# Last down projection of a two-block transformer: 16 of its 44 weight chunks as seven block products

## The reference

```python
        f = rms_norm_2(h, ffn_norm_g[i])
        h = h + (jax.nn.silu(f @ ffn_w1[i]) * (f @ ffn_w3[i])) @ ffn_w2[i]
        h = h + (p[i] @ pl_w_up[i]) * jax.nn.sigmoid(h @ pl_w_gate[i])
    return rms_norm_2(h, final_norm_g)
```

## Time and profile before

| what | value |
|---|---|
| median of 3 runs | 2418.42 us (2418.24 to 2418.65) |
| span of the profiled execution, first to last instruction | 2417.2 us |
| PE busy | 2404.8 us, 99% |
| DVE busy | 1389.7 us, 57% |
| ACT busy | 1170.4 us, 48% |
| first matmul of `down2`, of `pg2` | 2081.40 us, 2320.76 us |

### The profile page before, as it was taken

One profiled execution on the slowest core, in us unless ns is written; L12 is line 12 of the kernel. 1 busy time (PEld: TensorE's weight loads), 2 busy tenths in 40 slices (PEclk: granted clock), 3 DMA queues, 4 the chain that ended last, 5 costly groups with the idle time before them and its releaser, 6 DMA issues.

```text
span 2417.2 us, 27743 instructions
## 1 busy us (share of the span) xinstructions
PE 2404.8 (99%) x10956; PEld 2000.9 (83%) x10956; DVE 1389.7 (57%) x1192; ACT 1170.4 (48%) x1110; POOL 127.4 (5%) x138
## 2 busy tenths in 40 slices
PE   9999999999999999999999999999999999999998
PEld 8888888888888888888888888888888888888886
DVE  6877645656666666544666474664545445444446
ACT  5554554656656556333455464454343433433335
POOL 5000000001111011000000000000010100100000
PEclk9999999999999999999999999999999999999999
DMA  7566556587777778755698855776766767666663
GB/s 257 187 205 204 167 179 199 179 301 237 234 243 252 235 235 253 276 205 193 202 299 279 254 174 175 231 245 211 230 211 214 221 208 226 231 225 213 213 229 123
DMA packets 276834, 535.16 MB, mean 221 GB/s; under 512 B 12634, under 2 KB 47376, under 8 KB 275856
## 3 DMA queue, kind: packets, MB, share of 16 engines
q1 hardware_dynamic: 276304, 533.21, 68.0%
q10 hardware_dynamic: 448, 0.79, 0.1%
HBM read 495.15 MB, written 39.59 MB: 221 GB/s over the span
## 4 chain that ended last, share of the span: by engine, by line
PE 99%; ACT 1%; DVE 0%; DMA 0%; issue 0%; DVEq 0%; SPq 0%; ACTq 0%
PE ps L1462 31%; PE ps L1464 31%; PE ps L1463 31%; PE ps L1455 2%; PE ps L1456 1%; PE ps L1700 1%; PE ps L1438 0%; PE ps L1715 0%; DMA h<-in_x_dram 0%; ACT w_hi L819 0%; PE ps L1840 0%; PE ps L1684 0%; PE ps L1721 0%; PE ps L1751 0%; DVE w_lo L1898 0%; ACT g_work L984 0%
## 5 line engine op out<-in xcount | busy, mean ns | idle before, releaser
L1898 DVE TENSOR_TENSOR w_lo<-raw,w_hi 128x2048 fp32r<-128x2048 f32 x424 | 980.5, 2312 | 986.4 <-ACT w_hi L819 986.1
L819 ACT ACTIVATE w_hi<-raw 128x2048 fp32r<-128x2048 f32 x424 | 812.8, 1917 | 1207.7 <-PE ps L1464 1168.5
L1462 PE MATMUL ps<-w_hi,xa 128*128 128x512 f32 x1856 | 723.6, 390 | 0.0
L1464 PE MATMUL ps<-w_hi,xa 128*128 128x512 f32 x1856 | 722.2, 389 | 0.0
L1463 PE MATMUL ps<-w_lo,xa 128*128 128x512 f32 x1856 | 722.1, 389 | 0.0
L1462 PE MATMUL ps<-w_hi,g 128*128 128x512 f32 x1408 | 549.2, 390 | 0.0
L1464 PE MATMUL ps<-w_hi,g 128*128 128x512 f32 x1408 | 547.9, 389 | 0.0
L1463 PE MATMUL ps<-w_lo,g 128*128 128x512 f32 x1408 | 547.8, 389 | 0.0
L1464 PEld LDWEIGHTS ps<-w_hi,xa 128*128 128x128 f32 x1856 | 348.4, 188 | 72.7
L1462 PEld LDWEIGHTS ps<-w_hi,xa 128*128 128x128 f32 x1856 | 348.4, 188 | 72.4 <-DVE w_lo L1905 0.2
L1463 PEld LDWEIGHTS ps<-w_lo,xa 128*128 128x128 f32 x1856 | 348.4, 188 | 71.8
(11 more groups left out here) (315 smaller groups left out, 997.6 us busy)
## 6 DMA issues: line engine op xcount, KB each, us to landing
raw<-in_ffn_w_dram SPq DMA_DIRECT2D x132, 1024.0 KB, 5.2
raw<-in_w_in_dram SPq DMA_DIRECT2D x94, 1024.0 KB, 5.2
raw<-in_w_up_dram SPq DMA_DIRECT2D x88, 1024.0 KB, 5.9
raw<-in_w_down_dram SPq DMA_DIRECT2D x44, 1024.0 KB, 5.4
raw<-in_w_out_dram SPq DMA_DIRECT2D x32, 1024.0 KB, 5.1
raw<-in_w_pg_dram SPq DMA_DIRECT2D x16, 1024.0 KB, 7.2
raw<-in_pl_w_gate_dram SPq DMA_DIRECT2D x16, 1024.0 KB, 6.0
up_turned_rows<-h SPq DMA_DIRECT2D x22, 512.0 KB, 3.0
```

Of the source, the lines that this page charges most:

```text
L819: A(w_hi[j % SPLIT][:, :], raw[s][:, :], ACT.Copy).then_inc(sem("w_hi_ready"), 1)
L1462: mm(o, high, hi, start=begin, stop=False)
L1464: return mm(o, low, hi, start=False, stop=end)
L1898: V.tensor_tensor(w_lo[j % SPLIT][:, :], raw[j % RAW][:, :], w_hi[j % SPLIT][:, :].bitcast(F32), ALU.subtract).then_inc(sem("w_lo_ready"), 1)
```

## The change

Of the 22 chunks of `down2` and of `down2b`, chunks 3, 5, 7, ... 17 (eight in each phase) are multiplied by Strassen's scheme. A chunk is now two k-tiles by 1024 columns in every chunk of these phases (before: four k-tiles by 512 columns), that is a 2x2 grid of 128x512 weight blocks, and the two k-tiles by two halves of tokens are a 2x2 grid of 128x128 activation blocks. In Winograd's form of the scheme the grid product takes seven block products in place of eight: 21 matmuls in place of 24. The first of these products is summed in bank 4, others in 5, 6 and 7, and those that belong to one output only go straight into banks 0 to 2.

The block sums that the scheme needs are made in three places:

- Weight sums, for each of the 16 chunks on DVE: `early_sums` (1024 wide), `late_sums` (two of 512; one overwrites a block of `raw` in place), then ACT rounds the three sums (`sums_high`, 1536 wide) and DVE makes their low part (`low_sums`, 1536 wide). The rounding of the chunk itself now waits for the first of the late sums.
- Activation sums ("forms"), once for each of eight k-tile pairs, in steps 1 to 8 of `glu`: four sums of 128x128 on POOL, rounded on ACT, low part on POOL, put in DRAM by SP. In `down2` and again in `down2b` SP loads 512 KB of them for each seven-product chunk; PE waits for them after its second product.
- Output sums, once a phase: a copy on ACT, eight additions of 128x512 on DVE at chunks 17 and 18.

Because both halves of the columns now grow together, both are finished only at the end of a phase: `add_pair` takes the place of `add_rows`, and PE starts the next phase when the halves are read. `turn_h` of quarters 0 and 1 moves into `down2b`, quarters 2 and 3 to its end, their takes into `pg2`; the 2 MB of `take_second` moves from `down2` to `pg2`. Some semaphores are merged under common names.

In the diff below, the first `paired`, the wait and transfer of the forms and the three tables of puts and takes are SP's; `seven` is in ACT's `high`; `seven_products` is PE's; the rest is DVE's.

```diff
+SEVEN = {"down2": (3, 5, 7, 9, 11, 13, 15, 17), "down2b": (3, 5, 7, 9, 11, 13, 15, 17)}
...
+            def paired(ph, w, c0, at):
+                for j in range(plan[ph]["body"]):
+                    if j in at:
+                        at[j]()
+                    load(ph, 0, j, weight(w, 2 * j, 2, c0, 1024))
+                    if j - 2 in SEVEN[ph]:
+                        take_forms(ph, j - 2)
...
+                sp.wait_ge(sem("chunks_multiplied"), chunk_no(ph, 0, c - 4) + 1 if n >= 2 else plan[ph]["chunk"])
+                sp.dma_start(form_factors[ph][n % 2].bitcast(F32), forms_dram[:, first:first + 1024]).then_inc(sem(f"forms_landed{n % 2}"), 16)
...
-            columns("down2", [(w, 0), (w, 512)], 1024, kts=FT,
-                    at={6: lambda i: put_blocks(plan["glu"]["iters"]), 7: lambda i: take_blocks(plan["glu"]["iters"]),
-                        8: take_second,
-                        16: lambda i: put_h_blocks("pg2", 0), 17: lambda i: take_h_blocks("pg2", 0)})
-            columns("down2b", [(w, 1024), (w, 1536)], 1024, kts=FT,
-                    at={5: lambda i: put_h_blocks("pg2", 1), 6: lambda i: take_h_blocks("pg2", 1),
-                        16: lambda i: put_h_blocks("pg2", 2), 17: lambda i: take_h_blocks("pg2", 2)})
+            paired("down2", w, 0,
+                   at={6: lambda: put_blocks(plan["glu"]["iters"]), 7: lambda: take_blocks(plan["glu"]["iters"])})
+            paired("down2b", w, 1024,
+                   at={8: lambda: put_h_blocks("pg2", 0), 9: lambda: take_h_blocks("pg2", 0),
+                       12: lambda: put_h_blocks("pg2", 1), 13: lambda: take_h_blocks("pg2", 1)})
             columns("pg2", [(t["pl_w_gate_2"][0], 0), (t["pl_w_gate_2"][0], 512)], 1024, peel=2,
-                    at={5: at_step(0, lambda: put_h_blocks("pg2", 3)),
-                        6: both(at_step(0, lambda: take_h_blocks("pg2", 3)), load_final_row)})
+                    at={0: at_step(1, lambda: take_h_blocks("pg2", 3)), 2: at_step(1, take_second),
+                        6: at_step(0, lambda: put_h_blocks("pg2", 2)),
+                        7: at_step(0, lambda: (take_h_blocks("pg2", 2), put_h_blocks("pg2", 3))), 5: at_step(1, lambda: load_final_row(0))})
...
+                seven = ph in SEVEN and i == 0 and j in SEVEN[ph]
+                if seven:
+                    act.wait_ge(sem("sums"), 3 * seven_no(ph, j) + 2)
                 A(w_hi[j % SPLIT][:, :], raw[s][:, :], ACT.Copy).then_inc(sem("w_hi_ready"), 1)
+                if seven:
+                    act.wait_ge(sem("sums"), 3 * seven_no(ph, j) + 3)
+                    A(sums_high[ph], sums[seven_no(ph, j) % 2], ACT.Copy).then_inc(sem("sums_high"), 1)
...
+            def seven_products(ph, j, hi, lo):
+                three(4, early[:, 0:P], early[:, S:S + P], block_(hi, 0), block_(lo, 0), begin, end)
+                three(0, late[:, 0:P], late[:, S:S + P], block_(hi, 2), block_(lo, 2), False, False)
+                pe.wait_ge(sem(f"forms_landed{n % 2}"), landed_forms(ph, n))
+                three(6, *form(1), block_(hi, 1), block_(lo, 1), begin, end)
+                three(2, *form(3), block_(hi, 3), block_(lo, 3), False, False)
+                pe.wait_ge(sem("sums_low"), no + 1)
+                hi, lo = sums_high[ph], sums_low[no % 2]
+                three(5, *form(0), block_(hi, 0), block_(lo, 0), begin, end)
+                three(7, *form(2), block_(hi, 1), block_(lo, 1), begin, end)
+                return three(1, late[:, P:S], late[:, S + P:2 * S], block_(hi, 2), block_(lo, 2), False, False)
...
+            def early_sums(ph, c):
+                dve.wait_ge(sem(f"raw_landed{c % RAW}"), landed_count(ph, c))
+                dve.wait_ge(sem("chunks_multiplied"), chunk_no(ph, 0, c - 4) + 1 if n >= 2 else plan[ph]["chunk"])
+                V.tensor_tensor(sums[no % 2][:, 0:1024].rearrange("p (k n) -> p k n", k=2), blocks[:, 1],
+                                raw[c % RAW][:, 0:1024].rearrange("p (k n) -> p k n", k=2), ALU.subtract).then_inc(sem("sums"), 1)
...
+            def paired(ph, n, at):
+                done_at = SEVEN[ph][-1]
+                for j in range(plan[ph]["body"]):
+                    if j == plan[ph]["body"] - 1:
+                        add_pair(ph, n)
+                    low(ph, 0, j + SPLIT)
+                    if j + SPLIT in SEVEN[ph]:
+                        low_sums(ph, j + SPLIT)
+                    if j == 0:
+                        early_sums(ph, 3)
+                    if j + 3 in SEVEN[ph]:
+                        late_sums(ph, j + 3)
+                    if j + 4 in SEVEN[ph] and j:
+                        early_sums(ph, j + 4)
+                    if j == done_at:
+                        merge_products(ph, n)
+                    if j == done_at + 1:
+                        add_products(ph, n)
+                    if j in at:
+                        at[j]()
+            paired("down2", 0, {})
+            paired("down2b", 2, {3: lambda: turn_h("pg2", 0), 6: lambda: staged_low("pg2", 0), 7: lambda: turn_h("pg2", 1),
+                                 10: lambda: staged_low("pg2", 1), 21: lambda: (turn_h("pg2", 2), turn_h("pg2", 3))})
```

More of the change, by code:

```diff
@@ L133, in two_blocks_program @@
         cols = sb("cols", [P, 434])
+        with nc.sbuf_tensor("forms_work", [P, 1024], F32) as forms_work:
+            pass
+        with nc.sbuf_tensor("forms", [P, 1024], F32R) as forms:
+            pass
         ident = sb("ident", [P, P])
@@ L140, in two_blocks_program @@
         with nc.sbuf_tensor("ff", [P, 16, S], F32) as ff:
+            pass
+        with nc.sbuf_tensor("ff_r", [P, 16 * S], F32R) as ff_r:
             pass
@@ L549, in h_block_dram @@
             def h_block_dram(ph, q):
-                return turned_dram if (ph, q) == ("pg1", 3) else up_turned_dram
+                return turned_dram if (ph, q) in (("pg1", 3), ("pg2", 3)) else up_turned_dram
             def put_h_blocks(ph, q):
@@ L1196, in earlier_glu, with form_high, glu_sixth @@
                     glu_high(i - 1)
+            def form_high(e):
+                act.wait_ge(sem("forms_summed"), e * 3)
+                A(forms[:, 0:512], forms_work[:, 512:1024], ACT.Copy).then_inc(sem("forms_high"), 1)
+            def glu_sixth(i):
+                if isinstance(i, int) and i == 0:
+                    silu_gate(0)
+                elif not isinstance(i, int) or i - 1 in FORM_TILES:
+                    form_high(i - 1)
             def earlier(f, n=1):
@@ L1389, in _ @@
                 0: steps({1: lambda: row_squares("out", 1)}),
+                1: steps({0: lambda: staged_high("pg2", 2)}),
                 3: steps({0: last_staged_high, 1: lambda: sigmoid("pg2", 2)}),
@@ new lines, in landed_forms, with paired @@
+            def landed_forms(ph, n):
+                before = len(range(n % 2, len(SEVEN["down2"]), 2)) if ph == "down2b" else 0
+                return 16 * (before + n // 2 + 1)
+            def paired(ph, name):
+                for j in range(plan[ph]["body"]):
+                    pe.wait_ge(sem(name), j // 2 + 1)
+                    pe.wait_ge(sem("w_lo_ready"), chunk_no(ph, 0, j) + 1)
+                    products = seven_products if j in SEVEN[ph] else eight_products
+                    products(ph, j, w_hi[j % SPLIT][:, :], w_lo[j % SPLIT][:, :]).then_inc(sem("chunks_multiplied"), 1)
```

255 lines of the change are left out of this document (185 added, 70 removed).

## The result

| kernel | median, us | runs | ratio to before, 95% |
|---|---|---|---|
| before | 2418.33 (2417.97 to 2418.65) | 4 | |
| after | 2439.79 (2438.46 to 2441.42) | 4 | 1.0089 [1.0074, 1.0103] |

Forecast: 2421.0 us, range 2410 to 2427. The changed kernel is 21.5 us slower than before, outside the range. The profiled execution took 2441.42 us, its span is 2439.7 us against 2417.2 us.

A forecast was written before the change was run, and what follows sets the result against it. PE, busy 99% of the span, was taken as the bound. The terms, -10.9 + 2.4 + 9.2 + 1.9 = +2.6 us, were added to 2418.4 us, giving 2421.0 us; range 2410 to 2427, likeliest case 2418.7 to 2424.3.

The forecast's parts named there:

- 16 chunks x 3 matmuls x 0.2267 us = 10.9 us: Seven-product chunks of `down2` and `down2b`: the removed matmuls on PE save 10.9 us.
- Rival D: PE doesn't get shorter because the new matmuls, through more banks, come slower than 0.2267 us: 2430 us, chance 0.03.
- The steady pairs: Pairs of chunks in the phases' steady part: PE takes 10.20 us, DVE's loop 9.92, so PE leads and nothing is lost.
- the 2.4 us of small stalls: DVE work at phase starts (0.26 us), phase ends (0.58) and transposes of quarters 0 and 1 (1.57) adds 2.4 us.
- rival C: DVE becomes the bound if each step has 0.1 us more, in steady pairs: about 2428 us, chance 0.07.
- Where SP is held up: `down2b`: puts waiting for transposes delay loads, so PE waits for forms at chunks 7 and 11, 4.6 us each, 9.2 us.
- Rival A: Transfers land in time and both forms stalls in `down2b` vanish: -8.5 us, 2409.9 us, chance 0.22.
- `pg2`, quarter 2: `pg2`: quarter 2's take goes out behind load 6, ACT waits, and the fifth chunk comes 1.9 us late (1 to 3).
- "nothing" for quarter 3: `pg2`: quarter 3 has one chunk more time than quarter 2, so it costs nothing.
- Rival B: PE's granted clock falls in the `down2b` stalls, from 4.4 us of idle on: 3 to 7 us more, 2426 us, chance 0.18.
- On POOL and in `glu`: nothing: `glu`: the added sums, at most 8.6 us of POOL in a step of 43.5 us, and SP's 512 KB puts cost nothing.
- The forms' loads: Forms' transfers, 3.0 us behind a chunk's load, arrive long before their chunk, except where SP is held up.

The follow-up runs named there:

- e6_eight: e4_all with three matmuls more in each seven-product chunk (last product added twice), so that all 44 chunks have 24: 2424.68 us.
- e3_puts: Changed kernel with the transposes of quarters 0 and 1 in `down2b` later in DVE's list, their puts and takes later in SP's: 2427.38 us.
- e2_turn3: Changed kernel with the last quarter's transposes no longer waiting for the put of the quarter before: 2438.00 us.
- e12_put5: e9 with the put of quarter 2 ahead of load 5 of `pg2`, no longer behind it: 2413.03 us.
- e5_filled: Changed kernel with useless matmuls on PE ahead of two waits, 11 in the first chunk of `down2` and 20 at chunk 2 of `pg2`: 2438.67 us.
- e10: e4_all with one long wait left in: the last quarter's transposes again wait for the put of the quarter before: 2419.90 us.
- e11: e10 with 20 useless matmuls on PE ahead of the wait at chunk 2 of `pg2`: 2417.78 us.
- e9: e4_all with the forms' transfers behind those of the rows in `glu` and `down2`: 2414.53 us.
- e13: e12_put5 with the low part of the last `glu` tiles made by DVE in place of POOL: 2412.20 us.
- e14_low_first: e13 with POOL's order in `glu` turned round, low parts before the four small form sums: 2410.37 us, ratio 0.9965.
- e4_all: Changed kernel with swapped banks, e2_turn3's and e3_puts' edits, and quarter 2's take in `pg2` straight behind its put: 2414.27 us, ratio 0.9984.

## Why the prediction was wrong

- **"16 chunks x 3 matmuls x 0.2267 us = 10.9 us"**: right in `down2`, by the count of matmuls and the 51.0 us for five pairs; 10.4 us by e6_eight. Rival D, slower starts, is out in `down2` and true in small in `down2b`: 0.233 us, some 1.2 us in all.
- **The steady pairs (10.20 against 9.92 us) and the 2.4 us of small stalls**: right; rival C is out.
- **"Where SP is held up", 9.2 us**: right in place and cause, and near in size at 8.4 us. e3_puts shows the cause. Rival A is out.
- **`pg2`, quarter 2, 1.9 us**: the number fitted by luck. e2_turn3 shows that 4.1 us stood there, and more was hidden by a wait that I did not have. My "nothing" for quarter 3 was the step that failed worst: I followed its put and its take, but not the wait inside `turn_h`, which ties DVE to the put of quarter 2, 5.14 us. That put, right behind a load, took 7.0 us to land; e12_put5 moved it ahead of the load, and it took 3.0.
- **The start of `down2`**: no sentence of the prediction is about it. The change needs the second column half's banks in chunk 0, before in chunk 11. The wait for them stood in the program already and had cost nothing; 3.15 us.
- **Rival B, the clock**: given 0.18, priced at 3 to 7 us more, and kept out of the sum at nothing. The mechanism holds (e5_filled, e10 and e11). With four gaps from 3.15 us on it cost 9.2 us. The prediction asked for 4.4 us of idle PE, the one fall that it had a row for; here the clock was at half behind gaps of 4.05 us and of 3.15 us too. (That row, 0.91 granted, means 82% of its half microsecond at full and not 91%, since the rest is at half; the 4.4 us stay.) The Trainium skill says, in "TensorE: Matmul & The Clock Gate", section "HAM oscillation — how this bites in real kernels", that a wait for a transfer in the middle of a kernel can put the clock back to half each time. These rows agree, by 0.58 granted behind the forms' wait at chunk 7.
- **"On POOL and in `glu`: nothing"**: 1.0 us in the profiled execution of after, and 1.6 us (8 steps of 0.2) in e9 to e13, until e14_low_first took it away. The added work was priced in busy time; it cost by where it lay, beside DVE's low part, and by 512 KB ahead of a put.
- **The forms' loads**: "long before their chunk" held, except behind SP's waits, as written.

The failure is one of coverage: the terms I priced came out at +1.7 us against +2.6, and what I had at nothing or not at all came out at 20.8 us. The range, 2410 to 2427, took the bounds of priced terms for the bounds of the result. The whole sequence of edits shows that the long waits and the half clock behind them are the cause of the slowdown: e4_all, without them, is 25.5 us faster than after. Not settled: why single runs scatter. Those of after lie within 3 us, those of before within 0.7 (four runs) to 1.7 us (27 runs). It is not the long waits: e4_all has none and scatters by 4.2 us, e12_put5 by 2.0, e13_dve_low by 1.4 and e14_low_first, in five runs, by 0.6. It shrank with the edits on transfers and on POOL, but which of them carries it was not singled out. A part lies outside the change: `glu` begins between 1601.9 and 1604.0 us in the traces, and no edit reaches what stands ahead of it.
